# Where the modulation columns sit in two post-norms, and where an odd tile's product is kept

## The chip, the cores and the metric

The kernel runs on one core of one Trainium2 chip. The metric is the device time of one execution in microseconds (us). The core has five engines with queues of their own: TensorE (PE; its weight loads are listed as PEld), VectorE (DVE), ScalarE (ACT), GpSimd (POOL) and SyncE (SP), which issues the DMAs here.

## The reference

Two blocks follow each other on a stream `x` of 512 tokens by 1024 features, batch 1. The change touches the first block and the entry to the second:

```python
# first block
mod = silu(c) @ ada_w + ada_b                  # six vectors: sh1 sc1 g1 sh2 sc2 g2
h = rms_norm(x, mix_pre_g) * (1 + sc1) + sh1
y = hybrid_mixer(h, ...)                       # attention and convolution, ends in "@ w_o"
x = x + g1 * rms_norm(y, mix_post_g)           # post-norm 1
h = rms_norm(x, ffn_pre_g) * (1 + sc2) + sh2
y = (silu(g) * u) @ w_ffn_out                  # g, u = split(h @ w_ffn_in)
x = x + g2 * rms_norm(y, ffn_post_g)           # post-norm 2
# second block: a Mamba-2 layer, then a stick-breaking attention layer
shift, scale, gate = split(silu(c_2) @ ada_w_2[0] + ada_b_2[0], 3)
h = rms_norm(x, norm_g_2[0]) * (1 + scale) + shift
...
```

## The kernel before, in words

Activations lie feature-major: `x`, `hhi` and `hlo` are 128 partitions by 8 tiles by 512 tokens. Every product is made in three passes of high and low parts (`hhi*whi`, `hlo*whi`, `hhi*wlo`). Weights come in panels of 128 x 2048; ACT makes `whi` (`split_hi`, L187) and DVE makes `wlo` (`split_lo`, L191) of each.

The modulation vectors `mod` take little part in the main stream. Their weights `ada` come in 56 chunks. POOL multiplies each chunk by the silu of `c` (L198) and adds it down to 128 x 256 (L207), which counts `acc_ready`. TensorE then adds over the partitions: two matmuls against a column of ones for each chunk (`columns`, L366 in a post-norm), which write two columns of PSUM bank 4 (`MODB`) and count `mod_done`. `read_mod` (L234) is the DVE instruction that waits for `mod_done` and adds the bias into `mod`.

A post-norm (`post_norm`, L321) takes the eight output tiles of a projection from the eight PSUM banks in the order `ORDER`. There are two of them, `post1` behind the mixer (chunks 12 to 19 are late for it, so `late` is 8 chunks) and `post2` behind the feed-forward (chunks 41 to 53, 13 chunks). Each does this:

1. First pass: ACT squares each bank (L378), TensorE adds the squares over the features (`token_sums`, L297, four matmuls for a tile), DVE scales the bank into `y` (L397). ACT takes the root (`token_std`, L305), DVE the reciprocal (`token_rs`, L311), and TensorE spreads the result over the partitions (`spread`, L317).
2. The loop over tiles in pairs: DVE multiplies tile `y` by the spread factor (L403). For the even tiles of the order POOL adds the product to `x` (L417), for the odd ones DVE does (L406). ACT squares each new `x` tile (L385), and `token_sums` adds those squares, in a ring of three square tiles.
3. The root, the reciprocal and a second `spread` follow for the next norm, and DVE does one `split_lo` between.

Then comes the pre-norm (`pre_norm`): DVE makes its coefficients (`coefs`, L427), DVE, ACT and DVE make `hhi` and `hlo` of each tile (L442, L451, L436), and TensorE starts the first panel of the next projection on each as it comes (L461).

Each engine's order is its program order. In the kernel before, the PE queue of a post-norm has the `columns` calls in six places, with these numbers of chunks:

```python
parts = [3, 3, 0, 0, 2, 0] if after == 0 else [3, 3, 1, 1, 2, after - 2]
```

The places are: before the first `spread`, after it, after the sums of tiles 2 and 5 of the loop, before the second `spread`, and after it. `post1` has 3, 3, 0, 0, 2, 0 and `post2` has 3, 3, 1, 1, 2, 3. `read_mod` is called on its own (`mods`), for `post1` right behind its DVE part, for `post2` behind the whole pre-norm. For odd tiles the product of L403 is written to a free PSUM bank (`SPARE`), from which L406 reads it.

Of the kernel before, what the change touches and what calls it, by code (L numbers as in the profile page):

```python
# [17 lines left out]
ALU = mybir.AluOpType  # L18
# [7 lines left out]
KT = D // P  # L26
# [74 lines left out]
def build(nc, x_in, panels, ada, vecs, cst, w_f, w_dt, x_kept, ac_rows, out):  # L101
    ctx = ExitStack()
    with ctx:
# [13 lines left out]
        x = sbuf(ctx, "x", [P, KT, S])  # L117
# [15 lines left out]
        ps = ctx.enter_context(nc.psum_tensor("ps", [P, 8, S], F32))  # L133
# [96 lines left out]
        def read_mod(e, a0, a1, bank=MODB):  # L230

            e.wait_ge(mod_done, a1)
            lo, hi = 2 * a0, 2 * a1
            e.tensor_tensor(mod[:, lo:hi], ps[:, bank, lo:hi], v("ada_b")[:, lo:hi], ALU.add).then_inc(mod_read, 1)  # L234
# [46 lines left out]
        rsq = sbuf(ctx, "rsq", [P, P])  # L281

        ORDER = [7, 6, 0, 1, 2, 3, 4, 5]
        SPARE = {1: 0, 3: 1, 5: 3, 7: 5}

        def counting(**used):

# [5 lines left out]
        def token_sums(pe, no, s, j, sq, bank):  # L293

            pe.wait_ge(*no("sq_ready", s * KT + j + 1))
            for b in range(TB):
                mm = pe.matmul(ps[32 * b:32 * b + 32, bank, 0:P], ones[:, 0:32],  # L297
                               sq[:, (s * KT + j) % sq.shape[1], b * P:(b + 1) * P], start=j == 0, stop=j == KT - 1,
                               skip_group_check=True)
            mm.then_inc(nsem["ss_used"], 1)  # L300
# [7 lines left out]
        def token_rs(dve, no, s):  # L308

            dve.wait_ge(*no("std_ready", s + 1))  # L310
            dve.reciprocal(rsq[:], rsq[:]).then_inc(nsem["rs_ready"], 1)  # L311

        def spread(pe, no, s, bank):

            pe.wait_ge(*no("rs_ready", s + 1))
            for b in range(TB):
                mm = pe.matmul(ps[:, bank, b * P:(b + 1) * P], ident[:, 32 * b:32 * b + 1].to_broadcast([P, P]), rsq[:],  # L317
                               start=True, stop=True)
            mm.then_inc(nsem["spread"], 1)

        def post_norm(post, gate, y, sq, last, late):  # L321

            N = nsem
            no = counting(bank_done=KT - 1, kept=KT, sq_ready=2 * KT, ss_used=2 * KT, std_ready=2, rs_ready=2, spread=2,
                          scaled=KT, x_new0=KT // 2, x_new1=KT // 2, coef_ready=1)

            def bank_written(e, j):
                if j < KT - 1:
                    e.wait_ge(*no("bank_done", j + 1))
                else:  # L330
                    e.wait_ge(panels_used, last + 1)

            def on_pe(pe, part):
                for j, b in enumerate(ORDER):
                    part(b).then_inc(N["bank_done"] if j < KT - 1 else panels_used, 1)
                    if j == 2:
                        pe.wait_ge(*no("kept", 1))
                        token_sums(pe, no, 0, 0, sq, ORDER[0])
                    if j >= 2:
                        token_sums(pe, no, 0, j - 1, sq, ORDER[0])  # L340
                token_sums(pe, no, 0, KT - 1, sq, ORDER[0])
                columns(pe, 0)
                spread(pe, no, 0, ORDER[0])
                columns(pe, 1)
                for j in range(KT):
                    token_sums(pe, no, 1, j, sq, ORDER[1])
                    if j in (2, 5):
                        columns(pe, 2 + j // 5)
                columns(pe, 4)
                spread(pe, no, 1, ORDER[1])  # L350
                columns(pe, 5)

            a0, a1, sums = late
            after = a1 - a0 - KT
            parts = [3, 3, 0, 0, 2, 0] if after == 0 else [3, 3, 1, 1, 2, after - 2]
            assert sum(parts) == a1 - a0

            def columns(pe, part):

                first = a0 + sum(parts[:part])  # L360
                for a in range(first, first + parts[part]):
                    if a == a0:
                        pe.wait_ge(*no("kept", KT - 1))
                    pe.wait_ge(acc_ready, a + 1)
                    for b in range(2):
                        mm = pe.matmul(ps[:, MODB, 2 * a + b:2 * a + b + 1], sums(a)[:, b * P:(b + 1) * P],  # L366
                                       ones[:, 0:1], start=True, stop=True)
                    mm.then_inc(mod_done, 1)

            def mods(dve):  # L370
                read_mod(dve, a0, a1)

            def on_act(act):
                for j, k in enumerate(ORDER):
                    bank_written(act, j)
                    if j >= 3:
                        act.wait_ge(*no("ss_used", j - 2))
                    act.activation(sq[:, j % 3, :], ps[:, k, :], ACT.Square).then_inc(N["sq_ready"], 1)  # L378
                token_std(act, no, 0, ORDER[0])
                split_hi(act, last + 2, 0)  # L380
                for j, k in enumerate(ORDER):
                    act.wait_ge(*no(f"x_new{j % 2}", j // 2 + 1))
                    if j >= 1:
                        act.wait_ge(*no("ss_used", KT + j - 2))
                    act.activation(sq[:, (KT + j) % 3, :], x[:, k, :], ACT.Square).then_inc(N["sq_ready"], 1)  # L385
                token_std(act, no, 1, ORDER[1])

            def coefs(dve):
                dve.tensor_tensor(coef[:, 0, :], v(post), m(gate), ALU.mult).then_inc(N["coef_ready"], 1)
                dve.wait_ge(*no("coef_ready", 1))  # L390

            def on_dve(dve):
                for j, k in enumerate(ORDER):
                    if j == 2:
                        split_lo(dve, last + 1, 0)
                    dve.wait_ge(*no("sq_ready", j + 1))
                    dve.tensor_scalar(y[:, k, :], ps[:, k, :], coef[:, 0, k:k + 1], None, ALU.mult).then_inc(N["kept"], 1)  # L397
                token_rs(dve, no, 0)
                dve.wait_ge(*no("kept", KT))
                dve.wait_ge(*no("spread", 1))  # L400
                for j, k in enumerate(ORDER):
                    part = ps[:, SPARE[j], :] if j % 2 else y[:, k, :]
                    dve.tensor_tensor(part, y[:, k, :], ps[:, ORDER[0], :], ALU.mult).then_inc(N["scaled"], 1)  # L403
                    if j % 2:
                        dve.wait_ge(*no("scaled", j + 1))
                        dve.tensor_tensor(x[:, k, :], x[:, k, :], part, ALU.add).then_inc(N["x_new1"], 1)  # L406
                split_lo(dve, last + 2, 0)
                token_rs(dve, no, 1)
                dve.wait_ge(*no("spread", 2))
                for r in range(2):  # L410
                    dve.wait_ge(*no(f"x_new{r}", KT // 2))

            def on_pool(pool):
                for j in range(0, KT, 2):
                    k = ORDER[j]
                    pool.wait_ge(*no("scaled", j + 1))
                    pool.tensor_tensor(x[:, k, :], x[:, k, :], y[:, k, :], ALU.add).then_inc(N["x_new0"], 1)  # L417

            return dict(pe=on_pe, act=on_act, coefs=coefs, mods=mods, dve=on_dve, pool=on_pool)

        def pre_norm(gain, sc, sh, thi, tlo, h0, rs, slot=1):

# [112 lines left out]
        with ExitStack() as seg:  # L535
            first = sbuf(seg, "first", [P, ADA_OWN, KT, 256])
# [141 lines left out]
        with ExitStack() as kept:  # L678
            macc = sbuf(kept, "macc", [P, 8, 256])

            with ExitStack() as seg:
# [30 lines left out]
                a0, w0 = ADA_FIRST, FIRST["wo"]  # L712
# [13 lines left out]
                for n in range(CT * CK):  # L726
                    at_hand = [j for j in left if left[j] < CK and n >= sum(DENSE_TAPS[:j])]
                    j = min(at_hand, key=lambda j: ((j, left[j] - 1) in TAPS[-1:], left[j]))
# [19 lines left out]
                post1 = post_norm("mix_post", "g1", y1, room[:, 0:3, :], w0 + 3, late=(12, 20, lambda a: macc[:, a - 12, :]))  # L748
                pre1 = pre_norm(v("ffn_pre"), "sc2", "sh2", hhi, hlo, room[:, 3:5, :], ps[:, ORDER[1], :])

                with nc.Block() as block:
# [291 lines left out]
                    def _(dve):  # L1043
# [106 lines left out]
                        dve.sem_inc(pair_free[0], 1)  # L1150
                        dve.sem_inc(pair_free[1], 2)
                        post1["dve"](dve)
                        post1["mods"](dve)
                        dve.wait_ge(mod_read, read_counts[(12, 20)])
                        pre1["coefs"](dve)
                        pre1["dve"](dve)
# [2 lines left out]
        with ExitStack() as kept:  # L1159
# [8 lines left out]
            with ExitStack() as seg:  # L1168
# [6 lines left out]
                c0, q0, a0 = FIRST["ffn_in"], 10, 20  # L1175
                parts = [(0, ADA_C2 - a0), (ADA_C2 - a0, FT - 1)]
# [48 lines left out]
                with nc.Block() as block:  # L1225
# [25 lines left out]
                    @block.vector  # L1251
                    def _(dve):
                        dve.wait_ge(mod_read, read_counts[(20, 41)])
                        post2["coefs"](dve)
                        stream(dve, "ffn_out", lo=True, keep_last=2)
                        post2["dve"](dve)
                        pre2["coefs"](dve)
                        pre2["dve"](dve)
                        post2["mods"](dve)

                    @block.tensor
                    def _(pe):
# [1098 lines left out]
```

## Time and profile before

| What | Value |
|---|---|
| Median of 3 runs | 1542.98 us (1541.76 to 1545.53) |
| Time of the profiled execution | 1542.98 us |
| Its span, first to last instruction | 1541.2 us |
| Mean granted TensorE clock | 0.933 of full speed |
| Busy: PE, PEld | 1384.4 us (90%), 1096.9 us (71%) |
| Busy: DVE, ACT, POOL | 934.0 us (61%), 549.1 us (36%), 557.1 us (36%) |

Busy time is summed over an engine's instructions and divided by the span. The two post-norms lie at 318 to 350 us and at 724 to 756 us of the span. A granted clock of 1.00 is 2.4 GHz, one of 0.50 is 1.2 GHz.

### The profile page before, as it was taken

The page shows a single profiled execution, that of the slowest core. Times are in us where ns is not written, and L with a number is a line of the kernel's source. Part 1 is how long each engine was busy: PE and PEld are TensorE (multiplying, and loading weights), DVE is VectorE, ACT ScalarE, POOL GpSimd, SP SyncE. Part 2 cuts the span into 40 slices and gives each one's busy share as a digit, 9 for nine tenths or more (in the row PEclk, how much of TensorE's full clock was granted, in tenths as well). Part 3 has the DMA queues.
Part 4 walks back from the last instruction along what each step waited for, and adds up shares of the span by engine and source line. Part 5 has one row for each costly group of instructions (what it writes and reads, how often), then busy time and mean ns, then how long its engine had stood idle before and what let it go on. Part 6 is the DMA issues. An engine that isn't in the chain of part 4 may idle for free. (4 is left out here: it accounts for less than half of the span.)

```text
span 1541.2 us, 18593 instructions
## 1 busy us (share of the span) xinstructions
PE 1384.4 (90%) x7392; PEld 1096.9 (71%) x7392; DVE 934.0 (61%) x1031; ACT 549.1 (36%) x697; POOL 557.1 (36%) x260
## 2 busy tenths in 40 slices
PE   2399987889999998999999979988699899999997
PEld 1278775667888887888778856765388689777775
DVE  6988866676665555323756646777882561355553
ACT  3122345533232222112354333444442332455541
POOL 3000004964998885999200003322200040122320
PEclk8599788988999999999799989998799999999998
DMA  9321211432554454454132233322313242111121
GB/s 380 125 83 57 108 47 64 138 136 82 189 192 164 188 193 191 164 194 187 55 137 85 82 97 110 101 85 68 117 55 105 103 158 100 55 55 55 55 82 55
DMA packets 41346, 181.04 MB, mean 117 GB/s; under 512 B 3392, under 2 KB 20160, under 8 KB 21312
## 3 DMA queue, kind: packets, MB, share of 16 engines
q1 hardware_dynamic: 41280, 180.12, 32.3%
q8 instruction: 46, 0.75, 0.2%
q14 instruction: 20, 0.16, 0.0%
HBM read 173.75 MB, written 6.36 MB: 117 GB/s over the span
## 5 line engine op out<-in xcount | busy, mean ns | idle before, releaser
L191 DVE TENSOR_TENSOR wlo<-raw,whi 128x2048 fp32r<-128x2048 f32 x95 | 265.6, 2797 | 179.8 <-ACT whi L187 177.0
L198 POOL TENSOR_TENSOR ada_raw<-ada_raw,cs 128x2048 f32<-128x2048 f32 x44 | 174.1, 3958 | 373.9 <-DVE cv L744 169.3
L253 PE MATMUL ps<-hhi,whi 128*128 128x512 f32 x640 | 251.7, 393 | 2.6 <-DVE wlo L191 1.0
L253 PE MATMUL ps<-hhi,wlo 128*128 128x512 f32 x640 | 249.4, 390 | 0.0
L253 PE MATMUL ps<-hlo,whi 128*128 128x512 f32 x640 | 249.1, 389 | 0.0
L187 ACT ACTIVATE whi<-raw 128x2048 fp32r<-128x2048 f32 x95 | 181.5, 1910 | 162.7 <-PE ps L1273 94.1
L207 POOL TENSOR_TENSOR ada_raw<-ada_raw 128x1024 f32<-128x1024 f32 x88 | 204.8, 2327 | 6.9
L1746 POOL TENSOR_TENSOR dec<-dec,cb 128x512 f32<-128x512 f32 x32 | 60.8, 1901 | 296.2 <-ACT dec L1712 296.2
L253 PEld LDWEIGHTS ps<-hhi,whi 128*128 128x128 f32 x640 | 120.2, 188 | 28.5 <-issue 2.8
L253 PEld LDWEIGHTS ps<-hhi,wlo 128*128 128x128 f32 x640 | 120.1, 188 | 25.8
L253 PEld LDWEIGHTS ps<-hlo,whi 128*128 128x128 f32 x640 | 120.2, 188 | 24.5
L1938 POOL TENSOR_TENSOR x<-x,rest 128x256 f32<-128x256 f32 (+3 forms) x32 | 49.0, 1532 | 164.7 <-DVE rest L2233 164.7
L2233 DVE TENSOR_TENSOR_SCAN rest<-rest,zero 128x128 f32<-128x128 f32 (+3 forms) x64 | 59.0, 962 | 55.4 <-ACT rest L2153 55.4
L744 DVE SCALAR_TENSOR_TENSOR cv<-u,vec,cv 128x512 f32<-128x512 f32 x120 | 81.8, 743 | 0.4
L1203 DVE TENSOR_TENSOR fg<-ps,fg 128x512 f32<-128x512 f32 x22 | 15.2, 692 | 102.2 <-ACT fg L1193 102.2
L1193 ACT ACTIVATE fg<-ps 128x512 f32<-128x512 f32 x22 | 13.2, 599 | 174.4 <-PE ps L253 174.4
L1273 PE MATMUL ps<-fhi,whi 128*128 (+1 forms) x176 | 70.2, 399 | 5.4 <-PEq L1177 5.4
L1367 DVE SCALAR_TENSOR_TENSOR xbc<-ps,vec,xbc 128x511 f32 (+5 forms) x72 | 48.7, 741 | 42.3 <-ACT xbc L1336 41.8
L1273 PE MATMUL ps<-fhi,wlo 128*128 (+1 forms) x176 | 70.3, 399 | 0.0
L1273 PE MATMUL ps<-flo,whi 128*128 (+1 forms) x176 | 70.0, 398 | 0.0
L1522 PE MATMUL ps<-hhi,whi 128*128 128x512 f32 x128 | 55.6, 434 | 0.0
L1522 PE MATMUL ps<-hlo,whi 128*128 128x512 f32 x128 | 51.9, 405 | 0.0
(369 smaller groups left out, 2922.8 us busy)
## 6 DMA issues: line engine op xcount, KB each, us to landing
raw<-panels SPq DMA_DIRECT2D x95, 1024.0 KB, 4.8
ada_raw<-ada SPq DMA_DIRECT2D x48, 1024.0 KB, 6.7
first<-ada SPq DMA_DIRECT2D x8, 1024.0 KB, 19.2
bc<-ac_rows SPq DMA_DIRECT2D x32, 256.0 KB, 4.5
x_kept<-x SPq DMA_DIRECT2D x2, 2048.0 KB, 9.4
x<-x_kept SPq DMA_DIRECT2D x2, 2048.0 KB, 8.6
x<-x_in SPq DMA_DIRECT2D x1, 2048.0 KB, 12.8
out<-y SPq DMA_DIRECT2D x8, 256.0 KB, 2.2
```

Of the source, the lines that this page charges most:

```text
L187: e.activation(whi[:, c % 2, :, :], raw[:, c % 2, :, :], ACT.Copy).then_inc(hi_split, 1)
L191: e.tensor_tensor(wlo[:, c % 2, :, :], raw[:, c % 2, :, :], whi[:, c % 2, :, :].bitcast(F32), ALU.subtract).then_inc(lo_split, 1)
L198: e.tensor_tensor(ada_raw[:, c % 2, :, :], ada_raw[:, c % 2, :, :], cs[:, which, :].unsqueeze(2).to_broadcast([P, KT, 256]), ALU.mult).the ...
L207: e.tensor_tensor((ada_acc[:, c % 2, :] if sums is None else sums).unsqueeze(1) if width == 1 else part, part, ada_raw[:, c % 2, width:2 * ...
L253: mm = e.matmul(ps[:, 2 * (qc % 2) + b, :], w[:, c % 2, 2 * k + b, :], src[part][:, k, :], **flags)
L744: dve.scalar_tensor_tensor(out=cv[:, j, :], in0=src, scalar=w, in1=cv[:, j, :], op0=ALU.mult, op1=ALU.add).then_inc(A["tap"], 1)
L1273: mm = pe.matmul(ps[:, b, :], w[:, c % 2, k2 * 8 + b, :], src[:, kt, :] if isinstance(i, int) else src[:, bass.ds(kt + i * 4, 1), :], star ...
L1367: ins = dve.scalar_tensor_tensor(out=xbc[:, bass.ds(t, 1), s:S], in0=ps[:, 2 * pair + b, 0:S - s], scalar=vec[:, bass.ds(wc, 1)], in1=xbc[ ...
L1522: mm = pe.matmul(ps[:, 2 * (qp % 2) + b, :], wt[:, cp % 2, 2 * kt + b, :], (hhi, hlo)[part][:, kt, :], start=(kt == 0 and j == 0), stop=(k ...
L1746: pool.tensor_tensor(dec[:, n % 2, :, :], dec[:, n % 2, :, :], cb[:, b // 2, :].unsqueeze(1).to_broadcast([P, HB, P]), ALU.mult).then_inc( ...
L1938: pool.tensor_tensor(sig[:, n % 3, :, 0:nk], sig[:, n % 3, :, 0:nk], rest[:, n % 2, :, S - nk + 1:S + 1], ALU.mult).then_inc(B["am"], 1)
L2233: scan = dve.tensor_tensor_scan(turned, turned, zero[:, 0:1].to_broadcast([P, nk]), 1.0, ALU.mult, ALU.add)
```

## The change

The changed kernel places the columns otherwise. None stands before the first `spread`. After it TensorE waits for all eight `kept` counts and does the chunks beyond eight (none in `post1`, five in `post2`). In the loop one chunk stands behind the sums of each of the tiles 0 to 6, and the last chunk stands behind the second `spread`. `read_mod` becomes a part of the post-norm's DVE program, behind the second reciprocal and before the coefficients of the pre-norm, for both post-norms. The product of an odd tile is written back to `y` in SBUF, and L406 adds `x` and `y`, both in SBUF.

```diff
-        SPARE = {1: 0, 3: 1, 5: 3, 7: 5}
...
                 token_sums(pe, no, 0, KT - 1, sq, ORDER[0])
-                columns(pe, 0)
                 spread(pe, no, 0, ORDER[0])
-                columns(pe, 1)
-                for j in range(KT):
-                    token_sums(pe, no, 1, j, sq, ORDER[1])
-                    if j in (2, 5):
-                        columns(pe, 2 + j // 5)
-                columns(pe, 4)
-                spread(pe, no, 1, ORDER[1])
-                columns(pe, 5)
-            a0, a1, sums = late
-            after = a1 - a0 - KT
-            parts = [3, 3, 0, 0, 2, 0] if after == 0 else [3, 3, 1, 1, 2, after - 2]
+                pe.wait_ge(*no("kept", KT))
+                a0, a1, sums = late
+                more = a1 - a0 - KT
+
+                def columns(a):
                     pe.wait_ge(acc_ready, a + 1)
                     for b in range(2):
                         mm = pe.matmul(ps[:, MODB, 2 * a + b:2 * a + b + 1], sums(a)[:, b * P:(b + 1) * P],
                                        ones[:, 0:1], start=True, stop=True)
                     mm.then_inc(mod_done, 1)
-            def mods(dve):
-                read_mod(dve, a0, a1)
+                for a in range(a0, a0 + more):
+                    columns(a)
+                for j in range(KT):
+                    token_sums(pe, no, 1, j, sq, ORDER[1])
+                    if a0 + more + j < a1 - 1:
+                        columns(a0 + more + j)
+                spread(pe, no, 1, ORDER[1])
+                columns(a1 - 1)
...
                 for j, k in enumerate(ORDER):
-                    part = ps[:, SPARE[j], :] if j % 2 else y[:, k, :]
-                    dve.tensor_tensor(part, y[:, k, :], ps[:, ORDER[0], :], ALU.mult).then_inc(N["scaled"], 1)
+                    dve.tensor_tensor(y[:, k, :], y[:, k, :], ps[:, ORDER[0], :], ALU.mult).then_inc(N["scaled"], 1)
                     if j % 2:
                         dve.wait_ge(*no("scaled", j + 1))
-                        dve.tensor_tensor(x[:, k, :], x[:, k, :], part, ALU.add).then_inc(N["x_new1"], 1)
+                        dve.tensor_tensor(x[:, k, :], x[:, k, :], y[:, k, :], ALU.add).then_inc(N["x_new1"], 1)
                 split_lo(dve, last + 2, 0)
                 token_rs(dve, no, 1)
+                read_mod(dve, late[0], late[1])
                 dve.wait_ge(*no("spread", 2))
...
                         post1["dve"](dve)
-                        post1["mods"](dve)
...
                         pre2["dve"](dve)
-                        post2["mods"](dve)
```

## Rows read from the trace of the kernel before

**Rows 1.** What PE waited for, 358 to 720 us: total us, times, longest.
```profile
PE ps L1273 <- PEq L1177: 5.4, 1, 5.4
PE ps L253 <- PEq L751: 0.7, 1, 0.7
```

**Rows 2.** Timeline of DVE in post-norm 1: start us, length us, instruction, idle before.
```profile
333.93 0.95 DVE L311 RECIPROCAL rsq<-rsq 128x128 f32<-128x128 f32 x1 [0.16 <-ACT rsq L305]
336.20 0.69 DVE L403 TENSOR_TENSOR y<-y,ps 128x512 f32<-128x512 f32 x1 [1.32 <-PE ps L317]
336.81 0.69 DVE L403 TENSOR_TENSOR ps<-y,ps 128x512 f32<-128x512 f32 x1
337.53 0.69 DVE L406 TENSOR_TENSOR x<-x,ps 128x512 f32<-128x512 f32 x1
338.14 0.68 DVE L403 TENSOR_TENSOR y<-y,ps 128x512 f32<-128x512 f32 x1
...
349.66 0.17 DVE L234 TENSOR_TENSOR mod<-ps,vec 128x16 f32<-128x16 f32 x1 [2.33 <-PE ps L317]
349.87 0.17 DVE L427 SCALAR_TENSOR_TENSOR coef<-mod,vec 128x8 f32<-128x8 f32 x1
```

**Rows 3.** Timeline of PE in post-norm 1, merged runs.
```profile
334.94 1.16 PE L317 MATMUL ps<-rsq,consts 128*128 128x128 f32 x8
...
338.95 1.17 PE L297 MATMUL ps<-pm,consts 128*32 128x128 f32 x16 [1.63 <-ACT pm L385]
...
345.84 1.87 PE L366 MATMUL ps<-consts,macc 128*128 128x1 f32 x8
347.57 2.05 PE L317 MATMUL ps<-rsq,consts 128*128 128x128 f32 x8
352.51 0.76 PE L461 MATMUL ps<-hhi,whi 128*128 128x512 f32 x1 [2.88 <-DVE hlo L436]
```

**Rows 4.** Timeline of ACT in post-norm 1.
```profile
345.98 0.37 ACT L305 ACTIVATE rsq<-ps,eps 128x128 f32<-128x128 f32 x1 [0.77 <-PE ps L297]
```

**Rows 5.** Timeline of POOL in post-norm 1.
```profile
336.97 1.27 POOL L417 TENSOR_TENSOR x<-x,y 128x512 f32<-128x512 f32 x1 [9.08 <-DVE y L403]
```

**Rows 6.** Timeline of PE in post-norm 2, merged runs.
```profile
741.85 1.40 PE L366 MATMUL ps<-consts,macc 128*128 128x1 f32 x12
744.88 1.17 PE L297 MATMUL ps<-y_place,consts 128*32 128x128 f32 x16 [1.63 <-ACT y_place L385]
...
747.40 1.01 PE L366 MATMUL ps<-consts,macc 128*128 128x1 f32 x4
748.35 1.57 PE L297 MATMUL ps<-y_place,consts 128*32 128x128 f32 x24
749.85 1.01 PE L366 MATMUL ps<-consts,macc 128*128 128x1 f32 x4
750.79 1.08 PE L297 MATMUL ps<-y_place,consts 128*32 128x128 f32 x16
...
758.26 0.76 PE L461 MATMUL ps<-hhi,whi 128*128 128x512 f32 x1 [0.33 <-DVE hlo L436]
```

**Rows 7.** Timeline of DVE in post-norm 2.
```profile
755.62 0.17 DVE L427 SCALAR_TENSOR_TENSOR coef<-mod,vec 128x8 f32<-128x8 f32 x1 [2.33 <-PE ps L317]
```

**Rows 8.** Busy time by stretch; PEclk is the granted clock.
```profile
336.00:338.00 2.00, 1.33 (x13) 1.24 (x12) 1.76 (x3) 0.00 (x0) 1.03 (x1) 0.81 0.00 0
356.00:358.00 2.00, 2.00 (x7) 1.53 (x6) 1.97 (x4) 1.20 (x2) 0.00 (x0) 0.57 0.00 0
...
752.00:754.00 2.00, 2.00 (x10) 2.00 (x11) 1.07 (x2) 0.31 (x1) 0.00 (x0) 0.50 0.43 86
```

**Rows 9.** Groups by line, DVE, 366 to 700 us: busy us, mean ns.
```profile
L389 DVE TENSOR_TENSOR coef<-vec,mod 128x8 f32<-128x8 f32 x1 | 3.6, 3609 | 0.7 <-PEq L1177 0.7
```

**Rows 10.** Timeline of DVE and POOL at the end of the feed-forward.
```profile
727.78 3.60 POOL L198 TENSOR_TENSOR ada_raw<-ada_raw,cs 128x2048 f32<-128x2048 f32 x1
...
728.29 5.24 DVE L191 TENSOR_TENSOR wlo<-raw,whi 128x2048 fp32r<-128x2048 f32 x1
```

More of the change, by code:

```diff
@@ L341, in on_pe @@
                 token_sums(pe, no, 0, KT - 1, sq, ORDER[0])
-                columns(pe, 0)
                 spread(pe, no, 0, ORDER[0])
-                columns(pe, 1)
-                for j in range(KT):
-                    token_sums(pe, no, 1, j, sq, ORDER[1])
-                    if j in (2, 5):
-                        columns(pe, 2 + j // 5)
-                columns(pe, 4)
-                spread(pe, no, 1, ORDER[1])
-                columns(pe, 5)
-            a0, a1, sums = late
-            after = a1 - a0 - KT
-            parts = [3, 3, 0, 0, 2, 0] if after == 0 else [3, 3, 1, 1, 2, after - 2]
[L356 to L363, printed above, removed]
+                pe.wait_ge(*no("kept", KT))
+                a0, a1, sums = late
+                more = a1 - a0 - KT
+                def columns(a):
                     pe.wait_ge(acc_ready, a + 1)
@@ L417, in on_pool @@
                     pool.tensor_tensor(x[:, k, :], x[:, k, :], y[:, k, :], ALU.add).then_inc(N["x_new0"], 1)
-            return dict(pe=on_pe, act=on_act, coefs=coefs, mods=mods, dve=on_dve, pool=on_pool)
+            return dict(pe=on_pe, act=on_act, coefs=coefs, dve=on_dve, pool=on_pool)
         def pre_norm(gain, sc, sh, thi, tlo, h0, rs, slot=1):
```

## The prediction

> **What bounds the kernel now.** I read the page first: PE is busy for 90% of the span, so what delays PE delays the end. The waits of PE come next. From 358 to 720 us, the feed-forward, PE waited only twice, for its own sequencer at the borders of blocks, 0.7 and 5.4 us [rows 1]. So whatever post-norm 1 loses is not caught up there; the panel loop has no slack that could take it in. The two post-norms are where PE does not set the pace. I therefore read the timelines of the five engines there, and the granted clock by stretch. In a post-norm the work goes round in a ring: DVE product, POOL or DVE add, ACT square, PE sums, ACT root, DVE reciprocal, PE spread, DVE pre-norm, PE panel. Any time added to that ring moves the first L461 matmul and everything behind it.
>
> **Where the loop stands before.** I call the start of the first L403 product t0. It is 336.20 us in post-norm 1 [rows 2]. A pair of tiles takes 338.14 - 336.20 = 1.94 us on DVE [rows 2]. The first sums start at t0 + 2.75 (338.95) [rows 3]. ACT starts the root at t0 + 9.78 (345.98) [rows 4]. The granted clock fell during 336 to 338 us (0.81 over that stretch) and came back in 356 to 358 us (0.57), after the panel had started at 352.51 [rows 3, 8]. So the whole loop, from its first sums on, runs at the lower level, 1.2 GHz.
>
> **Part 1, columns ahead of the first spread: removed, 0 us.** The reciprocal ended at 333.93 + 0.95 = 334.88 and the spread started at 334.94 [rows 2, 3]. The three chunks that stood there were covered by the root and the reciprocal, and only 0.06 us could be gained. The new wait for `kept` has nothing to wait for, since DVE made the last `y` before its reciprocal.
>
> **Part 2, columns behind the first spread.** `post1` now has none there. `post2` has five instead of three. Three chunks are 12 instructions in 1.40 us, about 0.117 us each, so five take 2.34 us at the upper level, from 741.85 to 744.2; the first sums came at 744.88 [rows 6]. If the clock falls midway, the last two cost 0.87 each instead of 0.47, which ends at 745.0. I take 0.1 us, with 0 and 0.9 as bounds.
>
> **Part 3, seven columns inside the loop. This is the main cost.** At the lower level one chunk takes 748.35 - 747.40 = 0.95 us from its start to that of the next work (750.79 - 749.85 = 0.94 again), and the sums of one tile take (749.85 - 748.35) / 3 = 0.50 us [rows 6]. A pair of tiles now needs 2 x 0.50 + 2 x 0.94 = 2.88 us of PE, against the 1.94 us in which DVE delivers a pair. PE becomes the bound of the loop. Its ladder: first sums at t0 + 2.75, then seven steps of 0.50 + 0.94 = 1.44 us, so the last sums start at t0 + 12.83. In post-norm 2 the last two sums start at 750.79, and take 1.08 us [rows 6]; half of it later, at 751.3, the last one starts, and with 0.64 us to the root (0.50 of work and the hand-over) the root comes at t0 + 13.47. Before it was t0 + 9.78. Cost: 3.7 us in each post-norm.
>
> **Part 4, the odd product in SBUF.** Before, L406 read `x` from SBUF and the product from PSUM, and ran beside POOL's add without loss: POOL's L417 ran from 336.97 to 338.24, DVE's L406 from 337.53 for 0.69 us [rows 2, 5]. Now both inputs of L406 lie in SBUF. What the trace shows of such instructions beside POOL: the coefficient at L389, 8 elements a partition, two SBUF inputs, took 3.609 us [rows 9], where the like-sized L427 took 0.17 at a time when POOL was idle [rows 2]. And the L191 that started at 728.29 ended at 733.53, 2.15 us after POOL's L198 ended (727.78 + 3.60 = 731.38) [rows 10]. DVE seems to stand until POOL's instruction is over. So the new L406 would start at t0 + 2.04 instead of t0 + 1.33, and a pair takes about 0.7 us longer, 2.6 us. That is still under PE's 2.88: the sums of tile 2 are ready at t0 + 2.75 + 2.6 = 5.35 and PE gets to them at 5.63. This cost lies hidden behind part 3. If part 3's cost is not there, it is the bound, about 2 us in each post-norm. The Trainium skill ("SBUF — State Buffer", section "SBUF: two separate sides") says the same: the port pair that VectorE and GpSimd share is an exclusive lock, which an instruction with two SBUF inputs needs and for which the loser waits in full. By that rule the add of each pair loses the race, since POOL starts first; by the rows of two instructions that overlapped without loss before, it would cost nothing, and the sum would be the same, since PE's ladder is longer.
>
> **Part 5, the second spread and `read_mod`.** Before, two chunks stood ahead of the second spread. The spread started 347.57 - 345.98 = 1.59 us after the root [rows 3, 4]; the first, which had no such delay, started 0.06 us behind its reciprocal, which is 1.41 us behind the root's start if the 0.95 and 0.37 us instructions and their hand-overs are the same. Gain: 0.15 us. Behind the spread the last chunk now counts, since `read_mod` waits for it and the pre-norm's coefficients stand behind `read_mod` in DVE's queue. Two chunks back to back took 347.57 - 345.84 = 1.73 us, so one adds 0.86 us [rows 3]. In `post1` `read_mod` was on the path already. In `post2` it is new there: 349.87 - 349.66 = 0.21 us [rows 2], where now 755.62 begins with the coefficients [rows 7]; its removal from behind the pre-norm gives nothing, as PE does not wait for it.
>
> **Sum.** Post-norm 1: 3.7 - 0.15 + 0.86 = 4.4 us. Post-norm 2: 0.1 + 3.7 - 0.15 + 0.86 + 0.21 = 4.7 us. Together 9.1 us. The profiled execution took 1542.98 us, 1.78 more than its span, and it is itself the median. Forecast: 1542.98 + 9.1 = 1552.1 us, 0.6% slower. The total count of columns, POOL's work and the DMAs stay as they are.
>
> **Rivals.**
>
> *The clock stays up or comes back inside the loop, not slower (0.06).* PE is now without a gap from t0 + 2.75 to the end of the loop. If that brought the clock back, a chunk would cost 0.47 and a tile's sums 0.3 us, and the loop would be DVE's again: the root at about t0 + 11.8, 2.0 us late. The spread would take 1.16 instead of 2.05 us [rows 3], which with the last chunk makes -0.4 us. The panel, which ran 5 us at half speed (352.51 to about 357.6) [rows 3, 8], would win 2.6 us. Sum: 2.0 - 0.15 - 0.4 - 2.6 = -1.15 in each, so 1540.9 us. It decides where the clock returns before the second spread. Against it: from 747.40 on, PE worked at just such a mixture, and in 752 to 754 us it was busy for all of 2.00 us at a granted clock of 0.50 [rows 6, 8]. The Trainium skill ("TensorE: Matmul & The Clock Gate", section "Why this matters for your kernels") advises to keep TensorE continuously busy to get the full clock, which would speak for this rival; the trace does not agree for matmuls of one column.
>
> *The clock falls, but only after part of the loop, or PE overlaps columns and sums better (0.10).* Then DVE's lock of part 4 bounds the loop: 2.0 - 0.15 + 0.7 = 2.55 in each, 1548.3 us with the small terms of `post2`. For it: the instant of the fall is not tied to the program.
>
> *Part of the delay is taken in later (0.07).* If PE's next stage waited for something that is not late, a panel or a chunk, one post-norm's 4.4 us would vanish: 1547.6 us, or no change if both did. Against it stand [rows 1] for the first; in `post2` PE's first panel waits for DVE's `hlo` [rows 6], which is late with it.
>
> *Contention is dearer (0.12).* If the lock also holds POOL's add or the next product, a pair takes 3.2 us or more: the last even sums come at t0 + 12.35, then 1.44 us, a root at t0 + 14.4, 0.95 later in each: 1554 us. A later return of the clock adds up to some 0.9 us a post-norm.
>
> **How the numbers follow.** The forecast has 0.65. Its own range, from the clock's instants and part 2, is 1550 to 1554 us. A measurement of this kernel can tell about 0.3%, 4.6 us, from no change. The range of 8 in 10 reaches down to the lock-bound case and up to the dearer contention: 1547.5 to 1555 us. Slower by over 0.3% (above 1547.6): the forecast, the dearer case, the lock-bound one and half of the absorbed one, 0.89. Within 0.3%: 0.09. Faster: 0.02.
>
> **What would show it.** In the changed profile: PE in the loop with gaps of almost nothing and a step of 1.44 us for each tile; the root (L305) near t0 + 13.5 in both post-norms; L406 at about 1.3 us or longer instead of 0.69, ending after POOL's L417; L234 about 2.9 us after the start of the second spread; L461 starting some 4.4 us later in post-norm 1 and 9 us later in post-norm 2; the clock at 0.50 through the loop. A loop at a clock of 1.00, a root nearer to t0 + 12, or a wait of PE that shrinks in the next stage would make the prediction wrong.

## The result, and the profile after

The changed kernel takes 1551.42 us (median of 5 runs, 1550.5 to 1554.28) against 1543.78 us for the kernel before (5 runs, 1541.76 to 1545.94). The ratio is 1.0053, with a 95% interval of 1.0037 to 1.0069: 5.7 to 10.7 us slower. The forecast was 1552.1 us, and slower. (The ratios here are those on record, taken from all runs; they differ from the quotients of the medians by at most 0.0007.)

The spans of the profiled executions are 1541.2 and 1550.4 us. PE's busy time went from 1384.4 to 1390.1 us with the same 7392 instructions. What PE waited for in the feed-forward is the same two block borders as before [rows 1]:

```profile
PE ps L1259 <- PEq L1164: 5.4, 1, 5.4
PE ps L253 <- PEq L739: 0.7, 1, 0.7
```

So nothing was taken in there, and the difference lies in the post-norms. The line numbers are lower than in the kernel before from L297 on: `token_sums` is L296, the root L304, the reciprocal L310, the spread L316, `columns` L349, the product L390, the DVE add L393, POOL's add L405, `coefs` L415, the panel L449.

The timeline of PE in post-norm 1 of the changed kernel, to set beside [rows 3] (start us, length us):

```profile
333.80 1.16 PE L316 MATMUL ps<-rsq,consts 128*128 128x128 f32 x8 [1.47 <-DVE rsq L310]
337.91 0.65 PE L296 MATMUL ps<-pm,consts 128*32 128x128 f32 x8 [2.95 <-ACT pm L373]
338.49 1.01 PE L349 MATMUL ps<-consts,macc 128*128 128x1 f32 x4
339.44 0.65 PE L296 MATMUL ps<-pm,consts 128*32 128x128 f32 x8
...
348.60 0.65 PE L296 MATMUL ps<-pm,consts 128*32 128x128 f32 x8
350.72 2.08 PE L316 MATMUL ps<-rsq,consts 128*128 128x128 f32 x8 [1.47 <-DVE rsq L310]
352.59 0.85 PE L349 MATMUL ps<-consts,macc 128*128 128x1 f32 x4
356.44 0.77 PE L449 MATMUL ps<-hhi,whi 128*128 128x512 f32 x1 [2.99 <-DVE hlo L424]
```

The reader is to see the ladder. From 337.91 to 348.60 the rows of sums and of columns take turns without a gap, seven steps of (348.60 - 337.91) / 7 = 1.53 us. In the kernel before, PE waited 0.75 us in each pair of this loop.

DVE, ACT and POOL in the same place (three timelines):

```profile
335.07 1.28 DVE L390 TENSOR_TENSOR y<-y,ps 128x512 f32<-128x512 f32 x2 [1.33 <-PE ps L316]
336.39 1.26 DVE L393 TENSOR_TENSOR x<-x,y 128x512 f32<-128x512 f32 x1
337.57 1.27 DVE L390 TENSOR_TENSOR y<-y,ps 128x512 f32<-128x512 f32 x2
...
345.06 2.28 DVE L191 TENSOR_TENSOR wlo<-raw,whi 128x2048 fp32r<-128x2048 f32 x1
...
353.48 0.17 DVE L234 TENSOR_TENSOR mod<-ps,vec 128x16 f32<-128x16 f32 x1 [2.81 <-PE ps L349]
353.80 0.17 DVE L415 SCALAR_TENSOR_TENSOR coef<-mod,vec 128x8 f32<-128x8 f32 x1
```

```profile
349.31 0.37 ACT L304 ACTIVATE rsq<-ps,eps 128x128 f32<-128x128 f32 x1 [3.52 <-PE ps L296]
```

```profile
335.83 1.26 POOL L405 TENSOR_TENSOR x<-x,y 128x512 f32<-128x512 f32 x1 [8.29 <-DVE y L390]
```

DVE's add takes 1.26 us instead of 0.69 [rows 2] and ends at 337.65, 0.56 us after POOL's add (335.83 + 1.26 = 337.09). A pair takes 337.57 - 335.07 = 2.50 us. But DVE is through with its loop and with the low part of the panel at 345.06 + 2.28 = 347.34, and the root starts only at 349.31, behind PE's sums: DVE's longer pair is not what the root waits for. The granted clock was 0.50 from 336 us until the panel ran. Each line gives a stretch in us, its length, the busy time (and number of instructions) of PE, PEld, DVE, ACT and POOL, then the granted clock, the DMA share and GB/s:

```profile
340.00:342.00 2.00, 2.00 (x19) 1.58 (x15) 1.97 (x4) 0.81 (x2) 1.18 (x1) 0.50 0.00 0
...
362.00:364.00 2.00, 2.00 (x9) 1.58 (x9) 1.93 (x4) 0.89 (x2) 0.00 (x0) 0.89 0.00 0
```

The same figures for both post-norms, counted from t0, the start of the first product (335.07 and 746.62 us in the changed kernel, 336.20 and 742.12 in the one before):

| us from t0 | before, 1 | after, 1 | before, 2 | after, 2 |
|---|---|---|---|---|
| root starts | 9.78 | 14.24 | 9.82 | 14.16 |
| second spread starts | 11.37 | 15.65 | 11.41 | 15.57 |
| coefficients start | 13.67 | 18.73 | 13.50 | 18.44 |
| first matmul of the panel | 16.31 | 21.37 | 16.14 | 21.08 |

That is 5.06 and 4.94 us later, 10.0 together. The spans differ by 9.2, since t0 of post-norm 1 itself came 1.13 us earlier, the work between the panel's start and the second t0 took 0.57 us longer, and what follows the second panel's start took 0.24 us less. Over the ten kernels of this study the first of these t0 lay between 334.71 and 337.53 us, although the first spread stood 1.40 or 1.41 us behind its root in all of them. What moves it ahead of that stays open; a us or two of every single span can therefore not be put down to the change.

### The profile page after: what moved, and what is told of

Same layout as the page of the kernel before. It is cut to its first block and busy times, and to the rows that moved or that the text cites. A ratio compares the mean times of both kernels' runs of the same rounds, so it can differ in the third digit from the quotient of the medians.

```text
span 1550.4 us, 18593 instructions
## 1 busy us (share of the span) xinstructions
PE 1390.1 (90%) x7392; PEld 1102.5 (71%) x7392; DVE 938.6 (61%) x1031; ACT 549.5 (35%) x697; POOL 556.6 (36%) x260
```

## The experiments

Eight kernels ran. The times of a kernel before are those taken beside them on the same chip.

**e1: the columns alone.** The changed kernel, with the odd product in PSUM again:

```diff
+        SPARE = {1: 0, 3: 1, 5: 3, 7: 5}
...
-                    dve.tensor_tensor(y[:, k, :], y[:, k, :], ps[:, ORDER[0], :], ALU.mult).then_inc(N["scaled"], 1)
+                    part = ps[:, SPARE[j], :] if j % 2 else y[:, k, :]
+                    dve.tensor_tensor(part, y[:, k, :], ps[:, ORDER[0], :], ALU.mult).then_inc(N["scaled"], 1)
...
-                        dve.tensor_tensor(x[:, k, :], x[:, k, :], y[:, k, :], ALU.add).then_inc(N["x_new1"], 1)
+                        dve.tensor_tensor(x[:, k, :], x[:, k, :], part, ALU.add).then_inc(N["x_new1"], 1)
```

> The changed kernel with one part undone: the product of an odd tile goes to a free PSUM bank again, as before the change. Theory (the columns in the loop bound it, through PE): PE still steps by 1.53 us a tile, the root comes 14.2 us after the first product, and the time is that of the changed kernel, 1551.4 us, within 1 us; DVE's pair of tiles goes back from 2.50 to 1.94 us and nobody gains by it. Rival (VectorE's longer pair carries the loss): the root comes at about 10 to 11 us and the time is 1544 to 1546 us.

Measured: 1551.32 us against 1542.05, ratio 1.0053 (1.0035 to 1.0072), the ratio of the whole change. DVE's pair was back at 1.94 us, and the root came 350.73 - 336.48 = 14.25 us after t0. The rows of PE in its post-norm 1:

```profile
345.42 0.65 PE L297 MATMUL ps<-pm,consts 128*32 128x128 f32 x8
346.01 1.01 PE L350 MATMUL ps<-consts,macc 128*128 128x1 f32 x4
346.95 0.65 PE L297 MATMUL ps<-pm,consts 128*32 128x128 f32 x8
```

Sums and chunk take 0.59 + 0.94 us here as in the changed kernel. The theory held: the placement of the columns (the loop, and the last chunk and `read_mod` behind the second spread) carries the whole loss.

**e2: the product in SBUF alone.**

```diff
-                    part = ps[:, SPARE[j], :] if j % 2 else y[:, k, :]
+                    part = y[:, k, :]
```

> The kernel before with one part of the change: the product of an odd tile is written to SBUF, the columns stay where they were. Theory (the add stands until POOL's add is over, and nothing hides it now): L406 takes 1.27 us and a pair 2.50 us; the last sums come 1.7 us later; the reciprocal then has to wait for the low part of a panel (2.28 us on DVE) and starts at about 12.3 us after the first product instead of 10.2, so 2.1 us in each post-norm, 4.2 us in all: 1547.5 to 1548 us. Rival (the lock is a detail without weight): 1543 to 1544.5 us. Rival (the two parts add up, each with half): also about 1547, but then the run with the columns alone would be 1547 too.

Measured: 1545.07 us against 1542.05, ratio 1.0014 (1.0001 to 1.0028), so 0.2 to 4.3 us. The trace shows the steps that were expected, and what they cost:

```profile
335.62 1.28 DVE L403 TENSOR_TENSOR y<-y,ps 128x512 f32<-128x512 f32 x2 [1.33 <-PE ps L317]
336.94 1.26 DVE L406 TENSOR_TENSOR x<-x,y 128x512 f32<-128x512 f32 x1
...
347.80 0.94 DVE L311 RECIPROCAL rsq<-rsq 128x128 f32<-128x128 f32 x1
```

The add takes 1.26 us, the reciprocal starts 12.18 us after t0 and directly behind the low part of the panel, and the panel's first matmul comes 18.13 and 17.93 us after t0, 1.8 us later in each post-norm. My 2.1 us was a little high: the reciprocal is 2.0 us later than before (10.18), and the 0.18 us by which PE's two chunks had held the spread before are gone. The measured time lies between the 1547.5 to 1548 us that I expected and the rival's 1543 to 1544.5, so it meets neither; the 3.6 us of the two panels still lie inside the interval. So the product's place costs some 3.6 us by the trace when it is alone, and nothing measurable on top of the columns (e1 against the whole change): the two costs don't add, they lie beside each other.

**e3: three chunks in the loop instead of seven.** The kernel before, with this placement:

```diff
-            parts = [3, 3, 0, 0, 2, 0] if after == 0 else [3, 3, 1, 1, 2, after - 2]
+            parts = [3, 2, 1, 1, 1, 0, 0] if after == 0 else [3, 5, 1, 1, 1, 0, after - 3]
...
-                    if j in (2, 5):
-                        columns(pe, 2 + j // 5)
+                    if j in (1, 3, 5):
+                        columns(pe, 2 + j // 2)
-                columns(pe, 4)
+                columns(pe, 5)
                 spread(pe, no, 1, ORDER[1])
-                columns(pe, 5)
+                columns(pe, 6)
```

> The kernel before with three chunks of columns in the loop, behind tiles 1, 3 and 5, and none ahead of the second spread; the others stand before and behind the first spread and, for post-norm 2, two behind the second. Theory (PE's ladder against DVE's pair): a pair needs 0.58 + 0.94 + 0.50 = 2.0 us of PE against 1.94 us of DVE, so the root comes 0.2 to 0.4 us later than before at most, the second spread starts 0.15 us nearer to its root, and the time is 1543 to 1544.5 us, that of before. Rival (each chunk in the loop costs its share): 3 of 7 chunks, 3.8 to 4 us, 1547.5 us.

Measured: 1540.51 us against 1542.05, ratio 0.9994 (0.998 to 1.0009). The root came 9.86 us after t0 in both (before: 9.78 and 9.82), the panel 16.22 and 16.01 us. PE of post-norm 1:

```profile
338.72 1.18 PE L297 MATMUL ps<-pm,consts 128*32 128x128 f32 x16 [2.08 <-ACT pm L385]
339.82 1.01 PE L366 MATMUL ps<-consts,macc 128*128 128x1 f32 x4
340.77 1.08 PE L297 MATMUL ps<-pm,consts 128*32 128x128 f32 x16
...
342.72 1.08 PE L297 MATMUL ps<-pm,consts 128*32 128x128 f32 x16
...
344.67 1.08 PE L297 MATMUL ps<-pm,consts 128*32 128x128 f32 x16
```

The first pair takes 340.77 - 338.72 = 2.05 us on PE and the next two 1.95 each, against 1.94 of DVE: the two engines are level, and the root is 0.04 to 0.08 us later than before, less than the 0.2 to 0.4 that I allowed. Three chunks there cost nothing that can be measured. (The time lies below the 1543 to 1544.5 us that I expected, but so does that of the kernel before beside it, and the ratio is 1 within its interval.) The cost is no price per chunk; it begins where PE's work for a pair passes DVE's, which the 2.50 us of DVE and 3.06 us of PE for a pair show from the other side.

**e7: the last chunk ahead of the second spread.** The changed kernel, with two lines exchanged:

```diff
-                spread(pe, no, 1, ORDER[1])
                 columns(a1 - 1)
+                spread(pe, no, 1, ORDER[1])
```

> The changed kernel with the last chunk of columns moved from behind the second spread to ahead of it, where PE waits 1.4 us for root and reciprocal; all else is as changed. Theory (read_mod waits for that chunk, and the pre-norm stands behind it): the chunk takes 0.95 us of the gap, the spread is not later, read_mod comes at 2.1 instead of 2.8 us after the spread's start, the first L449 matmul 0.7 to 0.9 us earlier in each post-norm, 1549.5 to 1550 us against 1551.4. Rival (read_mod is not on the path): L449 where it was, 1551.4 us.

Measured: 1550.23 us against 1543.35, ratio 1.0047 (1.0028 to 1.0065); the time alone can't tell it from the changed kernel. The trace can. `read_mod` ran right behind the reciprocal, and the coefficients no longer waited for it but for the spread:

```profile
352.24 0.11 DVE L234 TENSOR_TENSOR mod<-ps,vec 128x16 f32<-128x16 f32 x1
354.48 0.17 DVE L415 SCALAR_TENSOR_TENSOR coef<-mod,vec 128x8 f32<-128x8 f32 x1 [2.14 <-PE ps L316]
```

The root stood at 14.25 and 14.15 us, the panel came at 20.40 and 20.31 us, 0.97 and 0.77 us earlier than in the changed kernel. That is what the last chunk and `read_mod` together cost in front of the coefficients. The cost of the change is a little less in post-norm 1, where `read_mod` stood there before too: from the second spread to the coefficients it was 2.30 and 2.09 us in the kernel before, 3.08 and 2.87 in the changed one, 0.78 more in each.

**e5: the same ladder at the other clock.** The kernel of e1 with filler matmuls, which write PSUM bank 2 from the high part of a panel and are read by nobody:

```diff
+                pe.wait_ge(hi_split, last + 2)
+                pe.wait_ge(*no("kept", KT - 1))
+                filler(pe, 5)
                 spread(pe, no, 0, ORDER[0])
...
+                filler(pe, 11 if more == 0 else 3)
                 for j in range(KT):
                     token_sums(pe, no, 1, j, sq, ORDER[1])
+                    if j < KT - 1:
+                        filler(pe, 1)
...
+            def filler(pe, n):
+                for _ in range(n):
+                    pe.matmul(ps[:, 2, :], whi[:, (last + 1) % 2, 0, :], whi[:, (last + 1) % 2, 0:4, :],
+                              start=True, stop=True, skip_group_check=True)
```

> The kernel of e1 (the changed placement of the columns, odd product in PSUM) with filler matmuls of 128 x 512 on top, whose results nobody reads: 5 ahead of the first spread, 11 (post-norm 2: 3) behind it, 1 behind the sums of each tile of the loop but the last. PE does more in the loop than in e1. Theory (the ladder is dear because TensorE runs at the lower level there, and matmuls of one column don't bring the clock up while dense ones do): a chunk costs 0.47 and a tile's sums 0.3 us, so even with the filler's 0.23 a tile takes 1.0 us instead of 1.53; the root comes 10 to 11 us after the first product instead of 14.2; the second spread and the panel behind it run at the upper level. 1538 to 1544 us against 1551.3 of e1, if the clock stays up through the loop in both; half of that if in one. Rival (the number of PE instructions is what costs, at whatever clock): the root at 15 us or later, 1552 to 1558 us.

Measured: 1546.34 us against 1543.35, ratio 1.0016 (1.0005 to 1.0027), some 5 us less than e1, although PE does more: 5 + 11 + 7 = 23 filler matmuls in post-norm 1 and 15 in post-norm 2. The loop in post-norm 1:

```profile
344.81 0.42 PE L297 MATMUL ps<-pm,consts 128*32 128x128 f32 x8
345.17 0.50 PE L371 MATMUL ps<-whi 128*128 128x512 f32 x1
345.51 0.50 PE L353 MATMUL ps<-consts,macc 128*128 128x1 f32 x4
345.94 0.43 PE L297 MATMUL ps<-pm,consts 128*32 128x128 f32 x8
```

```profile
342.00:344.00 2.00, 2.00 (x26) 1.52 (x25) 1.97 (x5) 1.24 (x4) 1.28 (x1) 1.00 0.00 0
```

The granted clock was 1.00 throughout the loop in both post-norms. A tile takes 345.94 - 344.81 = 1.13 us with a filler in it, against 1.53 without one at 0.50, and the root comes 11.15 and 11.12 us after t0 instead of 14.2. So PE's time for the ladder is a matter of the clock. Whether the fillers in the loop held it, or the 16 ahead of the loop (8 in post-norm 2), this run does not tell. The time missed my range by 2 us. I had a step of 1.0 us where it is 1.13, and behind the loop, where I had put no fillers, the clock fell: to 0.50 near 349 us in post-norm 1, so that the spread took 2.08 us, and at about 759 us in post-norm 2. The panels started at the lower level in both.

**e4, e6 and e8: fillers in the kernel before.** These ask what the lower clock costs the kernel before, and whether it can be had back. The fillers stand (first post-norm, second post-norm where it differs):

| | ahead of spread 1 | behind it | behind tiles 1, 3, 5 | ahead of spread 2 | behind it |
|---|---|---|---|---|---|
| e4 | 3 chunks | 3 chunks, 5 fillers | 4, 4, 4 fillers | 2 chunks, 1 filler | 10 fillers; 5 chunks, 4 fillers |
| e6 | 5 fillers; 3 chunks | 5 fillers, 3 chunks | 1 chunk and 3 fillers each | 2 chunks, 1 filler | 10 fillers; 2 chunks, 6 fillers |
| e8 | 5 fillers | 2 chunks, 7 fillers; 5 chunks, 2 fillers | 1, 1, 2 chunks and 3, 3, 1 fillers | 2 chunks, 1 filler | 11 fillers; 2 chunks, 8 fillers |

e4 also moves the two chunks that post-norm 2 had in its loop to behind the second spread. The core of its edit:

```diff
                 columns(pe, 1)
+                pe.wait_ge(hi_split, last + 2)
+                filler(pe, 5)
                 for j in range(KT):
                     token_sums(pe, no, 1, j, sq, ORDER[1])
-                    if j in (2, 5):
-                        columns(pe, 2 + j // 5)
+                    if j % 2 and j < KT - 1:
+                        filler(pe, 4)
```

> The kernel before with filler matmuls of 128 x 512 in PE's gaps of the two post-norms (5 ahead of the loop, 4 behind each odd tile, 1 ahead of the second spread, 10 or 4 behind it), whose results nobody reads; it does more work than the kernel before. It asks what the lower clock costs. If they keep the granted clock at 1.00: the second spread takes 1.16 instead of 2.05 us, the panel behind it runs at full speed (2.6 us less), 3.5 us less in each post-norm, 1536 us. If the clock falls all the same: each filler takes 0.43 us, 4 of them are longer than the gap of 0.75 us, a pair takes 2.7 instead of 1.94 us, 2.5 to 3 us more in each post-norm and 1 to 2 us for the last fillers, 1549 to 1552 us.

> The kernel before with the loop of e3 (a chunk behind tiles 1, 3 and 5) and with the fillers of e4 put more densely: post-norm 1 has 5 ahead of the first spread in place of the columns, 5 behind it, 3 behind each odd tile, 1 and 10 around the second spread; post-norm 2 has 5, 3, 1 and 6. If the clock never falls in either post-norm: 3.5 us less in each than the kernel before, 1535 to 1536 us. If it falls in the gaps where the columns stand and comes back in the loop, as in e4: about the time of e4, 1537 to 1538 us.

> The kernel before with the columns spread out (post-norm 1: 2 behind the first spread, 1, 1, 2 behind tiles 1, 3, 5, 2 ahead of the second spread; post-norm 2: 5, 1, 1, 2, 2 and 2 behind the second spread) and with fillers put so that PE has dense work from the last panel on: 5 ahead of the first spread as in e5, 7 or 2 behind it, 3, 3, 1 behind the odd tiles, 1 ahead of the second spread, 11 or 8 behind it. Their results are read by nobody. If e6 was slow because the clock fell in its first gaps and its longer PE program then ran at the lower level, this one keeps 1.00 from the last panel to the next: a pair stays at 1.94 us, the root comes 9.9 to 10.2 us after the first product, the panel runs at full speed: 3.5 us less in each post-norm than the kernel before, 1535 to 1537 us. If fillers cost whatever the clock is, it is as slow as e6, 1547 to 1548 us.

Measured: e4 1537.81 us against 1542.05, ratio 0.9967 (0.9955 to 0.9978). e6 1547.75 against 1543.35, ratio 1.0034 (1.0022 to 1.0045). e8 1543.53 against 1542.38, ratio 1.0011 (1.0001 to 1.0021). e4 beats both kernels; e6 and e8, which I held for improvements of it, do not, and both expectations failed. The granted clock by stretch, in post-norm 1 of e4:

```profile
334.00:336.00 2.00, 2.00 (x16) 2.00 (x14) 1.29 (x2) 0.20 (x1) 0.52 (x1) 0.70 0.00 0
336.00:338.00 2.00, 2.00 (x7) 1.71 (x8) 1.93 (x5) 1.15 (x2) 1.34 (x2) 0.50 0.00 0
...
340.00:342.00 2.00, 2.00 (x12) 1.26 (x16) 1.97 (x4) 0.96 (x2) 1.36 (x2) 0.59 0.00 0
342.00:344.00 2.00, 2.00 (x36) 1.25 (x28) 2.00 (x2) 1.15 (x2) 0.54 (x1) 1.00 0.04 8
...
352.00:354.00 2.00, 2.00 (x10) 1.57 (x9) 1.96 (x4) 1.20 (x2) 0.00 (x0) 1.00 0.00 0
```

The clock fell here too, and it did so while PE was busy: for 2.00 of the 2.00 us from 334 to 336 us, with chunks and a spread. But with four fillers and no chunk in a pair it was back at about 342 us and stayed for the second spread and the panel. The root came 11.25 us after t0 (1.5 us later than before, the price of fillers at the lower level), and the panel came 351.41 - 334.71 = 16.70 and ran at full speed. In post-norm 2 the root came at 9.63; there the five chunks behind the second spread were followed by another fall, and the panel ran its first 2.5 us at the lower level. So the expectation's first case came true in part, with 1537.81 us against 1536. The gain is not in the loops. The panels started 0.39 us later and 0.60 earlier than in the kernel before; but there they ran at the lower level for 4.8 and 5.3 us (the first shorter instruction starts at 357.34 and 763.52), here for none and 2.6. A matmul of the panel starts every 0.43 us at the lower level and every 0.23 at the upper, so that a stretch there costs about half its length, and these four terms make 4.0 us (an estimate), against 4.2 between the medians.

e6 shows what the same idea costs when it fails. Its pairs hold a chunk and only three fillers, and the clock stayed at 0.50 from 341 us to the end of the loop:

```profile
341.34 1.08 PE L297 MATMUL ps<-pm,consts 128*32 128x128 f32 x16
342.35 1.01 PE L379 MATMUL ps<-consts,macc 128*128 128x1 f32 x4
343.23 1.63 PE L363 MATMUL ps<-whi 128*128 128x512 f32 x3
344.79 1.08 PE L297 MATMUL ps<-pm,consts 128*32 128x128 f32 x16
```

```profile
344.00:346.00 2.00, 2.00 (x20) 0.93 (x19) 1.91 (x1) 0.83 (x2) 0.00 (x0) 0.50 0.00 0
```

A pair took 344.79 - 341.34 = 3.45 us on PE, and the root came 13.46 and 14.12 us after t0. In e8 the clock held until nearly 346 us in post-norm 1, where it fell with PE busy for 2.00 of 2.00 us, and the root came at 9.56 us; in post-norm 2 it fell at about 742 us, behind the five chunks, and the root came at 14.10 us. One post-norm won and the other lost. That each filler set's outcome follows its chunks is what these four post-norms look like; I did not separate it from chance in the moment of the fall, and two post-norms of each are few.

## Why the prediction was right

**What bounds the kernel.** Right. No wait in the feed-forward shrank, and the delay of post-norm 1 came through whole.

**Part 1, columns ahead of the first spread, 0 us.** Right. The spread stood 1.41 us behind its root and t0 1.27 us behind the spread, as before.

**Part 2, five chunks behind the first spread, 0.1 us.** Right within its bounds. They ran from 746.35 to 748.96, and the first sums at 749.37 waited 0.42 us for ACT, not for them.

**Part 3, seven chunks in the loop, 3.7 us in each.** The mechanism was right, and e1, e3 and e5 show it: alone it gives the whole loss, with PE's pair no longer than DVE's it gives none, and with the clock up it shrinks. The size was low: the root came 4.46 and 4.34 us later, at t0 + 14.24 and 14.16 where I had 13.47. The step of the ladder is 1.53 us, not 1.44. I had taken the 0.50 us of a tile's sums from three tiles in a row [rows 6]; with a chunk behind each, the sums of one tile take 0.58 us before the chunk starts. Seven steps of 0.09 us are 0.6 of the 0.7 to 0.8 us that were missing; in post-norm 1 the first sums also came at t0 + 2.84 instead of 2.75, and the way from the last sums to the root took 0.71 us instead of 0.64.

**Part 4, the odd product in SBUF.** Right: DVE's add stood until POOL's was over, in every pair, a pair took 2.50 us (forecast 2.6), and it lay hidden under PE's 3.06. The Trainium skill's rule of the exclusive port pair ("SBUF — State Buffer", section "SBUF: two separate sides") agrees with these rows and with those of e2. Its price without the cover was 1.8 us in each post-norm by e2's trace, near the 2 us that I gave. What the prediction left out there is that the reciprocal then also waits for the low part of the panel on DVE: in e2 the root came only 1.7 us later, the reciprocal 2.0.

**Part 5, the second spread and `read_mod`.** The gain at the spread was 0.18 us (1.41 us behind the root against 1.59; forecast 0.15). The last chunk cost 0.67 us up to `read_mod`, since it starts while the last spread matmul still runs, where I had put 0.86 behind it. From `read_mod` to the coefficients it was 0.32 and 0.11 us instead of 0.21. Together the coefficients came 0.78 us later behind the spread in each post-norm, against a forecast of 0.86 and 1.07.

**Sum.** 9.1 us were forecast, the traces show 10.0 in the two post-norms, and the measured ratio allows 5.7 to 10.7. The 0.7 to 0.8 us that part 3 missed in each are partly offset by parts 2 and 5. That 1551.42 us is only 0.7 from the forecast is in part luck: the medians differ by 7.6 us, not by 9.1, and the kernel before ran 0.8 us above the 1542.98 that the forecast starts from.

**The rivals.** That the clock comes back because PE has no gap did not happen: PE was busy for 2.00 of 2.00 us at 0.50 all through the loop. The lock-bound case is e2's, not this one's. Nothing was absorbed. The contention was not dearer than the lock, since POOL's add stayed at 1.27 us. That case also held a later return of the clock: from the panel's start to its first shorter instruction it was 5.7 and 4.0 us, against 4.8 and 5.3 before, so it came later in one post-norm and earlier in the other. The chances have a slip: the four cases named for a slower kernel add up to 0.905, where the text has 0.89.

## What to carry to other kernels

Work that is moved into another engine's gaps is free only up to the length of the gap at the clock that TensorE has there; add up the two engines' time for one step of the loop and compare, rather than price each piece. A short matmul costs twice as much in a stretch in which TensorE has dropped to 1.2 GHz (a chunk took 0.43 us in e5's loop and 0.94 in e1's), and being busy with sums and one-column matmuls did not bring the clock back here. Undo the parts of a change one at a time in both directions: the SBUF product cost 1.8 us a post-norm alone and nothing beside the columns, which neither run by itself would have told.

## What the runs showed of the hardware

The full clock can be bought with useless work, at times. With fillers of 512 columns the granted clock stayed at 1.00 through the loop of e5, where sums and chunks alone, with PE just as much without a gap, had 0.50. In e4, whose loops have no chunks, the clock came back within the loop, and the kernel before became faster by a ratio of 0.9967 (0.9955 to 0.9978). The Trainium skill ("TensorE: Matmul & The Clock Gate", section "Why this matters for your kernels") advises continuous work for that. The traces agree for the fillers of e4 and e5. They do not for the sums and the chunks of one column, with which PE was busy for 2.00 of 2.00 us at 0.50 in the changed kernel, nor for e6, where PE was as busy from 342 to 352 us, with three fillers in a pair, at 0.50. e5 has only two fillers in a pair and stayed at 1.00, but it entered its loop at 1.00; no run tells whether that made the difference. The purchase is a gamble: e6 paid for its fillers at the lower level and came out at 1.0034.

What an add on VectorE costs depends on where its operands lie while GpSimd works. With the product in PSUM it took 0.69 us beside POOL's add; with both inputs in SBUF it took 1.26 us and ended 0.56 us after POOL's.
